# The delta rule's inverse built in place of k and v, two gate tiles made during its preparation, and an output projection that begins with three attention halves

## The reference, cut to what matters

```python
q = l2_norm(q); k = l2_norm(k)                      # per head
kb = kc * bc[..., None]
a_mat = where(tril_strict, einsum('bhnid,bhnjd->bhnij', kb, kc) * decay, 0.0)
l_mat = a_mat + eye                                 # lower triangular
u = triangular_solve(l_mat, vc * bc[..., None])     # here: the inverse of l_mat, times this
w = triangular_solve(l_mat, kb * exp(gc)[..., None])
attn_intra = einsum('bhnid,bhnjd->bhnij', qc, kc) * decay
def step(state, inp):                               # the scan over the chunks
    v_new = u_i - einsum('bhck,bhkv->bhcv', w_i, state)
    o_i = einsum('bhck,bhkv->bhcv', qd_i, state) + einsum('bhij,bhjv->bhiv', a_i, v_new)
    state = state * gl_i[..., None, None] + einsum('bhck,bhcv->bhkv', kt_i, v_new)
y_dn = rms_norm(o, dn_norm_w) * silu(z)
y_att = dilated_attention(...) * silu(gate_att)
x = x + concat([y_dn, y_att]) @ w_out
```

## Time and profile before

| | us |
|---|---|
| median of 3 runs (1248.83 to 1252.34) | 1252.33 |
| the profiled execution's own time | 1250.68 |
| its span, first to last instruction | 1248.9 |
| PE busy | 1154.6 (92%) |
| DVE busy | 609.1 (49%) |
| ACT busy | 501.9 (40%) |
| POOL busy | 495.1 (40%) |

### The profile page before, as it was taken

How to read it: one execution, slowest core, us unless ns; L and a number is a source line. 1 busy time by engine, 2 the same in 40 slices (tenths; PEclk the granted TensorE clock), 3 DMA queues, 4 the chain that set the end, 5 groups by cost and what they waited for, 6 DMA issues and landing times.

```text
span 1248.9 us, 15616 instructions
## 1 busy us (share of the span) xinstructions
PE 1154.6 (92%) x5616; PEld 912.3 (73%) x5616; DVE 609.1 (49%) x1191; ACT 501.9 (40%) x826; POOL 495.1 (40%) x387
## 2 busy tenths in 40 slices
PE   6998999996798797999999998997999999989997
PEld 5775777674697575777777766875888888878886
DVE  4376887546673425356666666425433334320003
ACT  5446444365343326344434455425433233311124
POOL 4443332344322352433333232443444555534443
PEclk9998999989899898999999997998999999999999
DMA  8576465510120032334441221342233333322221
GB/s 170 135 158 133 124 135 129 142 34 1 49 88 1 15 117 85 99 121 135 137 129 56 68 68 34 102 135 84 68 101 101 91 85 93 101 101 69 99 67 68
DMA packets 114286, 116.32 MB, mean 93 GB/s; under 512 B 4817, under 2 KB 97191, under 8 KB 114228
## 3 DMA queue, kind: packets, MB, share of 16 engines
q1 hardware_dynamic: 98800, 86.58, 25.6%
q10 hardware_dynamic: 14212, 26.13, 6.6%
q0 software_dynamic: 1216, 2.83, 0.7%
HBM read 113.41 MB, written 2.12 MB: 93 GB/s over the span
## 4 chain that ended last, share of the span: by engine, by line
PE 85%; DVE 6%; ACT 4%; issue 1%; DMA 1%; POOL 1%; SPq 0%; ACTq 0%; DVEq 0%
PE bank L642 23%; PE bank L643 22%; PE bank L644 22%; PE bank L792 3%; PE bank L817 2%; PE bank L800 2%; PE bank L913 2%; PE bank L924 2%; DMA raw<-w_in 1%; PE bank L677 1%; PE bank L721 1%; PE bank L937 1%; DVE nhf L1570 1%; DVE h_lo L1502 1%; ACT whi L1158 1%
## 5 line engine op out<-in xcount | busy, mean ns | idle before, releaser
L448 POOL TENSOR_TENSOR wlo<-raw,whi 128x512 fp32r<-128x512 f32 x312 | 421.5, 1381 | 606.9 <-ACT whi L1158 606.8
L642 PE MATMUL bank<-h_hi,whi 128*128 128x512 f32 x1016 | 417.0, 410 | 26.1 <-DVE h_lo L1502 17.6
L643 PE MATMUL bank<-h_lo,whi 128*128 128x512 f32 x1016 | 400.8, 394 | 0.0
L644 PE MATMUL bank<-h_hi,wlo 128*128 128x512 f32 x1016 | 400.1, 394 | 0.0
L642 PEld LDWEIGHTS bank<-h_hi,whi 128*128 128x128 f32 x1016 | 194.0, 191 | 92.0 <-issue 37.0
L644 PEld LDWEIGHTS bank<-h_hi,wlo 128*128 128x128 f32 x1016 | 193.4, 190 | 42.4
L643 PEld LDWEIGHTS bank<-h_lo,whi 128*128 128x128 f32 x1016 | 194.0, 191 | 40.1 <-issue 3.4
L1158 ACT ACTIVATE whi<-raw 128x2048 fp32r<-128x2048 f32 (+1 forms) x79 | 150.2, 1901 | 174.4 <-PE bank L644 159.6
L1279 ACT ACTIVATE pT_a<-bank 128x256 f32<-128x256 f32 (+3 forms) x80 | 32.4, 405 | 195.1 <-PE bank L800 195.1
L642 PE MATMUL bank<-ffn_hi,whi 128*128 (+1 forms) x176 | 70.3, 399 | 4.1 <-DVE ffn_lo L1502 4.1
L1599 DVE SCALAR_TENSOR_TENSOR ada_acc<-ada_w,small,ada_acc 128x512 f32<-128x512 f32 x84 | 71.2, 848 | 0.0
(11 more groups left out here) (310 smaller groups left out, 1483.7 us busy)
## 6 DMA issues: line engine op xcount, KB each, us to landing
raw<-w_in SPq DMA_DIRECT2D x66, 512.0 KB, 5.6
ada_w<-w_ada ACTq DMA_DIRECT2D x96, 256.0 KB, 2.9
raw<-w_up SPq DMA_DIRECT2D x44, 512.0 KB, 4.6
raw<-w_down SPq DMA_DIRECT2D x22, 512.0 KB, 4.0
raw<-w_out SPq DMA_DIRECT2D x16, 512.0 KB, 4.5
x_tok<-x SPq DMA_DIRECT2D x4, 512.0 KB, 5.9
toe<-bias_rows POOLq DMA_DIRECT2D x8, 256.0 KB, 7.2
raw<-w_branch_swa SPq DMA_DIRECT2D x4, 512.0 KB, 3.5
```

Of the source, the lines that this page charges most:

```text
L448: ins = pool.tensor_tensor(wlo[s][:, c], raw[s][:, c], whi[s][:, c].bitcast(F32), ALU.subtract)
L642: pe.matmul(ps, wh, h_hi, start=start, stop=False)
L643: pe.matmul(ps, wh, h_lo, start=False, stop=False)
L644: return pe.matmul(ps, wl, h_hi, start=False, stop=stop)
```

## The change: what it does

- `X` and `XT` move into the tiles of v and k (each chunk's slice is overwritten once it has been transposed), `AT` and `P1` to where the first attention's k and v lay. The input `h_hi`, `h_lo` therefore stays intact during the preparation. POOL makes the diagonals of chunks 0 and 1 before the norm's squares, and no longer waits for tile 32.
- The gate tiles' steps are spread anew: two in each of the eight norm portions (tiles 29 and 30), and 16 more steps (tiles 31 and 32) in the preparation: 3 before chunk 0, and 3, 3, 3 and 4 inside chunks 0 to 3. Tiles 31 and 32 both use bank 3, and tile 32 waits for tile 31's eviction, which DVE does in chunk 1 behind `dn_qd`. `brow` has one bank (2) for all chunks.
- In the scan the outputs go to banks 6, 5, 4, 7, and the last chunk is multiplied by z and split by DVE rather than by POOL. ACT makes the attention's high parts before u and w rather than after.
- The output projection begins with the attention steps of three tiles (33, 34, 35), then their delta-rule steps, then tile 36 alone. `norm_sum` of tiles 33 to 36 comes behind the tiles of block 19 (T = 37, 38); ACT's list there is unchanged.

```diff
-        X = at("dn_X", [P, TT, DN_H, P], offset=split_at)[0]
-        XT = at("dn_XT", [P, TT, DN_H, P], offset=split_at + 8192)[0]
-        AT = at("dn_AT", [P, TT, DN_H, P], offset=split_at + 24576)[0]
-        P1 = at("dn_P1", [P, TT, DN_H, P], offset=split_at + 16384)[0]
+        X, XT = (qkv[:, f:f + 4, :].rearrange("p h (c i) -> p c h i", c=TT) for f in (8, 4))
+        AT = at("dn_AT", [P, TT, DN_H, P], offset=U + 49152)[0]
+        P1 = at("dn_P1", [P, TT, DN_H, P], offset=U + 57344)[0]
...
+            pool.wait_ge(S["att_pv"], 32)
...
+            diagonals(0)
+            diagonals(1)
             pool.wait_ge(S["dn_silu"], 2)
...
-            pool.wait_ge(S["tile_ready"], T_S1)
...
+            for c in (2, 3):
+                pool.wait_ge(S["dn_grow"], c - 1)
+                pool.wait_ge(S["dn_brow"], c - 1)
+                diagonals(c)
+                start_xt(pool, c - 2)
+            start_xt(pool, 2)
+            start_xt(pool, 3)
...
-            for e in range(TT):
+            for e in range(TT - 1):
...
+        SCAN_OUT = (6, 5, 4, 7)
...
-            return bank[T % 2]
+            return bank[{30: 7, 31: 3, 32: 3}.get(T, T % 2)]
...
-        norm_steps = lambda w: 128 + 4 * (w + 1)
+        norm_steps = lambda w: 130 + 2 * w if w < 8 else 144 + 3 * (w - 7) + w // 12
...
-                        evac(pe, T - 2)
+                        evac(pe, T - 2 if T != 32 else 31)
+                        if T == 30:
+                            pe.wait_ge(S["mod_add"], ADA_DN // 8)
...
             for w in range(8):
                 gate_steps(norm_steps, w)
+                if w == 4:
+                    grow(0)
...
-            broadcasts(0)
+            brow(0)
+            pe.wait_ge(S["nt_done"], 14)
+            gate_steps(norm_steps, 8)
             for c in range(TT):
...
                 if c + 1 < TT:
-                    broadcasts(c + 1)
+                    grow(c + 1)
+                gate_steps(norm_steps, 9 + c)
+                if c + 1 < TT:
+                    brow(c + 1)
...
-            for j in range(4):
-
-                gemm(N_S1 + j, T_S1 + 2 * j, ready=None if j else {4: (S["att_lo"], 4), 0: (S["dn_lo"], 4)})
-                for kt in (2 * j - 2, 2 * j - 1):
-                    if kt >= 0:
-                        norm_sum("n1", 2, kt)
+            first = [(T_S1 + k, N_S1 + k // 2, k % 2) for k in range(3)]
+            pe.wait_ge(S["att_lo"], 4)
+            for half in (1, 0):
+                if half == 0:
+                    pe.wait_ge(S["dn_lo"], 3)
+                    pe.wait_ge(S["dn_lo_last"], 1)
+                for T, n, u in first:
...
+                    for kt in range(4 * half, 4 * half + 4):
+                        mm = three(ring(T)[:, :], n % 2, kt * 256 + u * P, hh[:, kt, :], hl[:, kt, :], kt == 4, kt == 3)
...
+            gemm(N_S1 + 1, T_S1 + 3, (1,))
+            for j in range(2, 4):
+                gemm(N_S1 + j, T_S1 + 2 * j)
+                for kt in (range(4) if j == 2 else (4, 5)):
+                    norm_sum("n1", 2, kt)
...
-            dve.wait_ge(S["tile_ready"], 33)
...
                 dve.tensor_tensor(qkv[:, 0:4, tok], qkv[:, 0:4, tok], state[:, :, :], ALU.mult).then_inc(S["dn_qd"], 1)
+                gate_tiles(norm_steps, 9 + c)
                 dve.wait_ge(S["dn_a"], c + 1)
...
+                    if e == TT - 1:
+                        mx4, tok = four(mixf[e % 2][:, :]), slice(e * P, (e + 1) * P)
+                        dve.wait_ge(S["dn_scaled"], e + 1)
+                        dve.tensor_tensor(mx4, mx4, zs[:, 0:4, tok], ALU.mult).then_inc(S["dn_mix_last"], 1)
+                        dve.wait_ge(S["dn_hi"], e + 1)
+                        rest(hl[:, 0:4, tok], mx4, hh[:, 0:4, tok], "dn_lo_last")
```

More of the change, by code:

```diff
@@ L464, in _, with diagonals @@
                 lo(n)
+            def diagonals(c):
+                pool.tensor_tensor(P1[:, c % 2], over(gdec[:, 4 * c:4 * c + 4]), each(m(C_TRIU)), ALU.mult).then_inc(S["dn_gtri"], 1)
+                pool.tensor_tensor(P1[:, 2 + c % 2], over(beta[:, 4 * c:4 * c + 4]), each(ident), ALU.mult).then_inc(S["dn_gtri"], 1)
+            pool.wait_ge(S["att_pv"], 32)
+            pool.wait_ge(S["g_ready"], 1)
+            pool.wait_ge(S["in_masks"], 16)
+            diagonals(0)
+            diagonals(1)
             pool.wait_ge(S["dn_silu"], 2)
@@ L846, in head_sum, with grow, brow @@
                 pe.matmul(bank[2 + j % 4][:, :], m(C_ONE), nsq4[j % 4][:, :], start=True, stop=True).then_inc(S["sum_done"], 1)
+            def grow(c):
+                pe.wait_ge(S["dn_gtri"], 2 * c + 1)
+                if c < 2:
+                    evac(pe, 28 + c)
+                else:
+                    pe.wait_ge(S["dn_exp"], c - 1)
+                pe.matmul(bank[c % 2][:, :], m(C_ONE), P1[:, c % 2].rearrange("p h i -> p (h i)"), start=True, stop=True)\
+                    .then_inc(S["dn_grow"], 1)
+            def brow(c):
+                pe.wait_ge(S["dn_gtri"], 2 * c + 2)
+                if c == 0:
+                    pe.wait_ge(S["nt_done"], 13)
+                else:
+                    pe.wait_ge(S["dn_dtb"], c)
+                pe.matmul(bank[2][:, :], m(C_STRIL), P1[:, 2 + c % 2].rearrange("p h i -> p (h i)"),
+                          start=True, stop=True).then_inc(S["dn_brow"], 1)
             for w in range(8):
                 gate_steps(norm_steps, w)
+                if w == 4:
+                    grow(0)
                 if w == 0:
@@ L857, in _ @@
             head_sum(7)
-            def broadcasts(c):
-                pe.wait_ge(S["dn_gtri"], 2 * c + 2)
-                if c < 2:
-                    evac(pe, 32 - c)
-                    pe.wait_ge(S["nt_done"], 13 + c)
-                if c >= 2:
-                    pe.wait_ge(S["dn_exp"], c - 1)
-                    pe.wait_ge(S["dn_dtb"], c - 1)
-                pe.matmul(bank[c % 2][:, :], m(C_ONE), P1[:, c % 2].rearrange("p h i -> p (h i)"), start=True, stop=True)\
-                    .then_inc(S["dn_grow"], 1)
-                pe.matmul(bank[2 + c % 2][:, :], m(C_STRIL), P1[:, 2 + c % 2].rearrange("p h i -> p (h i)"),
-                          start=True, stop=True).then_inc(S["dn_brow"], 1)
-            broadcasts(0)
+            brow(0)
+            pe.wait_ge(S["nt_done"], 14)
+            gate_steps(norm_steps, 8)
             for c in range(TT):
@@ L1348, in _ @@
                 if l == 3:
+                    evac(act, 32)
                     act.activation(gate[:, :, :], gate[:, :, :], ACT.Silu).then_inc(S["gate_silu"], 1)
+            for p in range(4):
+                act.wait_ge(S["att_mix"], p + 1)
+                act.activation(hh[:, 4 + p, :], qk_att[:, p, :], ACT.Copy).then_inc(S["att_hi"], 1)
             act.preload_act_table_set("natural_log_exp_and_others")
@@ L1354, in _ @@
                 act.activation(kbe[:, c], four(bank[7][:, :]), ACT.Copy).then_inc(S["dn_w"], 1)
-            for p in range(4):
-                act.wait_ge(S["att_mix"], p + 1)
-                act.activation(hh[:, 4 + p, :], qk_att[:, p, :], ACT.Copy).then_inc(S["att_hi"], 1)
             for c in range(TT + 2):
@@ L1364, in _ @@
                         act.wait_ge(S["dn_osum"], c - 1)
-                    act.activation(Dk[c % 2][:, :, :], four(bank[4 + c][:, :]), ACT.Square).then_inc(S["dn_osq"], 1)
+                    act.activation(Dk[c % 2][:, :, :], four(bank[SCAN_OUT[c]][:, :]), ACT.Square).then_inc(S["dn_osq"], 1)
                 if 1 <= c <= TT:
@@ L1776, in _ @@
                 dve.wait_ge(S["dn_brow"], c + 1)
-                dve.tensor_tensor(attnT[:, c], four(bank[2 + c % 2][:, :]), Dk[c % 2][:, :, :], ALU.mult).then_inc(S["dn_dtb"], 1)
+                dve.tensor_tensor(attnT[:, c], four(bank[2][:, :]), Dk[c % 2][:, :, :], ALU.mult).then_inc(S["dn_dtb"], 1)
                 dve.wait_ge(S["dn_dtb"], c + 1)
```

29 lines of the change are left out of this document (11 added, 18 removed).

## The result

The changed kernel took 1257.32 us (median of 5 runs, 1256.72 to 1258.99), the kernel before 1251.72 us (5 runs, 1248.83 to 1252.34). Timed once more it was 1258.53 us and the ratio 1.0054 (1.0038 to 1.007). The forecast was 1255.8 us. The span of the profiled execution grew from 1248.9 to 1255.5 us.

A forecast was written before the change was run, and what follows sets the result against it. PE was taken as the bound, with gain only from its gaps. Norms and preparation +0.1, inverse -0.5, end of scan -1.3, output projection +5.1 gave +3.4 us: 1255.8 us against the 1252.33 us median; range 1250.5 to 1260.0 us, 8 in 10.

The forecast's parts named there:

- main term: Output projection: the late norm sums delay block 20's weights, so PE stands 6.4 us before block 20; +5.1 us in all.
- Norm phase: Norms before the preparation: new order ends earlier, though ACT stands before hi(17) waiting for tile 30; -4.9 us, bounds -6.5 and -3.5.
- Chunk 0: Preparation, first chunk: nine gate matmuls (2.05 us) go in front of transposition L903, where PE idled 1.29 us; +0.6 us.
- Chunk 1: Preparation, second chunk: tile 32's first step waits for tile 31's eviction, and X comes later; +4.0 us, ends 2.9 and 4.8.
- Chunk 2: Preparation, third chunk: gate steps find tile 32 open and finish over 1.5 us before ACT; no change.
- Chunk 3: Preparation, fourth chunk: twelve matmuls fit PE's idle 4.95 us, but the copy stands before X; +0.4 us.
- Inverse: Inverse after the preparation: same operations, strided slices cost nothing, clock may stay up at the start; -0.5 us.
- End of the scan: Last chunk's finish by DVE and ACT instead of POOL's low part lets the projection's second halves start earlier; -1.3 us.
- rival B: Clock falls in the short gaps too, before the second halves and in chunks 0 and 1; 1260.0 us, chance 0.20.
- Output projection: PE's start to block 20: 35.4 us, with waits of 0.8 and 6.4 us, then a slow-clock restart; +5.1 us.
- Rival A: Gate matmuls keep PE at the upper clock through the preparation and into the inverse; 1250.9 us, chance 0.22.
- rival C: Output projection: the wait for block 20's weights doesn't come, hidden or sums served sooner; 1247.8 us, chance 0.08.

## Why the prediction was right, and where it missed

**Direction and main term: right.** The forecast's likeliest case was the one that came, 1.5 us too low. As a difference the miss is larger: +5.6 us measured for +3.4, since the kernel before came out 0.6 us faster in five runs than in the three that the forecast stood on. By the prediction's own bound (1256.1 us) the result is slower, which it had at 0.45, just behind 0.47 for the same. Undoing the sums and adding them to the kernel before both gave the term its size from outside.

**Norm phase: forecast -4.9, came -4.2 (33.96 and 33.98 us in two traces, for 38.13).** The mechanism is the one named: ACT idle 3.92 us before hi(17), with tile 30's matmul as releaser (forecast about 4). The missing 0.7 us is less than seven traces with the same norm phase differ by (32.75 to 35.68 us). In the changed kernel's first trace, counted from the phase's start (0.9 us later there than before, for reasons ahead of the change), DVE's first norm operation behind hi(17) came 0.4 us later than I had it, and DVE's rest took 10.34 us for my 10.0, as its two operations beside POOL took 1.25 and 1.41 us. What I didn't see is how much lay there: with hi(17) last the norm phase is 6.6 us shorter, more than the wait and the operation together (3.92 + 1.9 us).

**Chunk 0: forecast +0.6, came +1.3 and +1.0.** The nine gate matmuls were priced right and ran at the upper clock: from the end of the last product to the transposition it took 3.78 us for 3.17, the forecast's 0.6. What I had left out stands beside them in the first trace. Behind 3.39 us of idle PE ran the products of chunk 0 mostly at the lower clock, 4.93 us where they had taken 4.37, and DVE's add beside POOL's diagonals took 1.53 us where it had taken 1.36.

**Chunk 1: forecast +4.0 with ends at 2.9 and 4.8, came +4.7.** PE stood for 4.37 us (forecast 4.2). From the copy's start to `X`, 5.04 us passed: 0.82 to PE's start, 1.42 for three matmuls, 1.70 for the row sum, 1.10 for the transposition. At the upper clock I had 2.9 us for this, so all of PE's work in it, and not a part, ran at the lower clock; the add behind then took 0.69 us where it had been 1.05. That the wait comes from tile 32's first step is shown: without this step in the chunk, it lasts 8.55 us.

**Chunk 2: nothing, as forecast (8.32 for 8.31 us). Chunk 3: forecast +0.4, came +1.2.** The copy is in it with 0.6 us; the missed part is DVE's add, 1.66 us where it took 0.73. In the timelines of the kernel before, DVE's and POOL's operations start in this order:

```profile
325.86 0.73 DVE L1787 TENSOR_TENSOR dn_X<-dn_X,mats 128x512 f32<-128x512 f32 x1
```

```profile
326.00 5.41 POOL L448 TENSOR_TENSOR wlo<-raw,whi 128x512 fp32r<-128x512 f32 x4
```

DVE was first by 0.14 us. After the change the copy pushes the add back to 328.90 us, and POOL's low part starts before it:

```profile
328.76 5.39 POOL L449 TENSOR_TENSOR wlo<-raw,whi 128x512 fp32r<-128x512 f32 x4
```

The Trainium skill, page "SBUF — State Buffer", section "Who interferes with whom", says that a VectorE operation with two inputs in SBUF contends with a GpSimd operation that reads SBUF, and that who issues first keeps the other waiting. The three traces agree: 0.73 us when DVE came first, 1.66 when POOL did, 0.69 when POOL was held back. I had used this rule for the product with z and not looked for it here.

**Inverse: forecast -0.5, came -1.5 in the first trace and 0.0 in the second.** Over all 14 traces it took 56.7 to 58.2 us for the same operations. Neither the forecast nor a gain is shown.

**End of the scan: forecast -1.3, came -1.1.** PE idled 1.64 us (forecast 2.1), and the clock stayed up, as forecast and against rival B.

**Output projection: forecast +5.1, came +5.5 and +4.7.** From PE's start to block 20's start I had 35.4 us; it took 35.68 and 35.57 (468.77 - 433.20 us). The waits of 0.8 and 6.4 us came as 0.64 and 6.33. This step is the one that made the change slower: without the late sums the change is level with before. The wait for hi(17) is no loss against before, where the norm phase was longer still, but a gain not taken. In two parts the end of the scan and the projection are -5.4 us for the attention halves and VectorE's finish, of which the end of the scan is 1.1, and +9.8 us for the sums.

**The sum.** Between the cuts +6.0 us came (+6.3 in the second trace) for +3.4. The norm phase, chunk 0, chunk 1 and chunk 3 each fell 0.7 to 0.8 us short in the first trace, all to the same side: in both chunks mostly the clock after a gap of 3 to 4 us, in chunk 3 DVE beside POOL, in the norm phase partly so. The inverse took 1.0 us of it back. One sign of the prediction failed: the inverse started at 330.62 us, not within 1.5 us of 326.6; 0.9 of these 4.0 us lie ahead of the norm phase. Rival A's condition, PE at the upper clock through the preparation, did not come (0.82); rival C's neither.

## What to carry to other kernels

A sum or a square that hands a buffer back is part of the queue of the engine that waits for this buffer: before it is moved later on TensorE, read what stands behind the waiting instruction on ScalarE. Here a weight block's conversion stood there, and two sums of 0.9 us each, moved 12 us later behind the next block, cost 9.8 us. The same holds for the conversion in the middle of the norms: put behind the last rsqrt, where nobody waits for it, it gave back 5.9 us. And fill a gap on TensorE only up to the first step that needs another engine's result: the step of tile 32 turned a gap of PE into a wait for an eviction; with this step in the next chunk the wait was gone (chunk 1 8.55 us for 13.00), though the whole kernel gained only about 3 us by it.
